# Two-block decoder of 256 tokens on one core: scores of 64-feature heads issued in pairs, filler work spread over the pairs, joined MLP products, gated outputs turned in parts

## The reference, cut to what matters

```python
# first block, layer 0: MoBA (8 heads of 64, ALiBi) beside forgetting attention (8 heads of 64)
s_own = einsum('bhqd,bhld->bhql', qc, ko) * Dh**-0.5 - slopes * rel_o        # causal, one block of 256
s_fox = einsum('bhqd,bhsd->bhqs', qb, k) * scale + cb[..., None] - c         # c = cumsum(log f)
y = concat([ya * silu(ga), yb * silu(gb)]);  x = x + y @ w_out_ab[j]
# first block, layer 1: differential attention (4 heads, two maps of 64, values of 128)
#   beside sliding-window attention with sinks (8 query heads of 64, 2 key heads)
x = x + y @ w_out_cd[j]
# second block, layer i = 0, 1: mixer (0: MLA, 1: stick-breaking), cross attention, MLP
h = h + mem_cross_attn(rmsnorm_2(h, norm_cross[i]), rmsnorm_2(mem, norm_mem[i]), ...)
h = h + square(relu(rmsnorm_2(h, norm_mlp[i]) @ w_in)) @ w_out               # 1024 -> 4096 -> 1024
```

## Time and profile before

| | |
|---|---|
| median of three runs | 1026.99 us (1026.68 to 1027.73) |
| the profiled execution: its time | 1027.6 us |
| the profiled execution: its span in the trace | 1025.8 us, mean granted clock of TensorE 0.985 |
| busy share of the span | PE 96%, PEld 86%, DVE 61%, ACT 53%, POOL 4% |
| DMA | 158.14 MB, mean 154 GB/s |

### The profile page before, as it was taken

How to read it: one execution, slowest core, us unless ns; L and a number is a source line. 1 busy time by engine, 2 the same in 40 slices (tenths; PEclk the granted TensorE clock), 3 DMA queues, 4 the chain that set the end, 5 groups by cost and what they waited for, 6 DMA issues and landing times.

```text
span 1025.8 us, 15748 instructions
## 1 busy us (share of the span) xinstructions
PE 989.2 (96%) x6172; PEld 879.7 (86%) x6172; DVE 627.6 (61%) x1208; ACT 548.2 (53%) x1029; POOL 38.3 (4%) x83
## 2 busy tenths in 40 slices
PE   8899999999999979999999999999999999999997
PEld 7677778787787979887999999899988889999995
DVE  5867545486864476656765555557873658455554
ACT  6575564366684445545744434455673557444352
POOL 4011000001130000000000000000000000000000
PEclk9899989999999989999999999999999999999999
DMA  9776312565332434343556565666435435565551
GB/s 288 218 164 124 124 41 88 163 202 164 123 114 62 122 90 150 124 128 121 182 186 200 173 201 176 235 164 177 152 103 185 146 104 195 176 203 171 198 186 42
DMA packets 114167, 158.14 MB, mean 154 GB/s; under 512 B 13783, under 2 KB 55085, under 8 KB 114093
## 3 DMA queue, kind: packets, MB, share of 16 engines
q1 hardware_dynamic: 113656, 156.56, 49.4%
q10 hardware_dynamic: 436, 0.56, 0.2%
HBM read 156.06 MB, written 1.05 MB: 153 GB/s over the span
## 4 chain that ended last, share of the span: by engine, by line
PE 84%; DVE 6%; ACT 4%; issue 2%; SPq 1%; DMA 1%; DVEq 0%; ACTq 0%
PE bank L475 24%; PE bank L476 24%; PE bank L477 24%; PE bank L613 3%; DVE w_lo L1771 2%; PE bank L638 2%; PE bank L627 2%; PE bank L607 1%; PE bank L529 1%; DMA raw<-in_w_in_ab 1%; ACT xT_hi L1319 1%; SPq L2472 1%; DVE xT_lo L1828 1%; ACT pb L1438 1%; PE bank L592 1%
## 5 line engine op out<-in xcount | busy, mean ns | idle before, releaser
L1771 DVE TENSOR_TENSOR w_lo<-raw,w_hi 128x1024 fp32r<-128x1024 f32 (+2 forms) x292 | 336.2, 1195 | 179.2 <-ACT w_hi L1274 178.9
L1274 ACT CAST w_hi<-raw 128x1024 fp32r<-128x1024 f32 (+2 forms) x292 | 283.4, 1027 | 146.6 <-DMA raw<-in_mlp_w_in 74.2
L475 PE MATMUL bank<-xT_hi,w_hi 128*128 128x256 f32 x784 | 224.5, 286 | 3.0 <-DVE xT_lo L1828 2.0
L476 PE MATMUL bank<-xT_lo,w_hi 128*128 128x256 f32 x784 | 222.5, 284 | 0.0
L477 PE MATMUL bank<-xT_hi,w_lo 128*128 128x256 f32 x784 | 222.5, 284 | 0.0
L475 PE MATMUL bank<-w_hi,xT_hi 128*128 128x512 f32 (+1 forms) x432 | 161.8, 375 | 9.0 <-issue 4.0
L477 PE MATMUL bank<-w_hi,xT_lo 128*128 128x512 f32 (+1 forms) x432 | 157.9, 365 | 0.0
L476 PE MATMUL bank<-w_lo,xT_hi 128*128 128x512 f32 (+1 forms) x432 | 157.8, 365 | 0.0
L475 PEld LDWEIGHTS bank<-xT_hi,w_hi 128*128 128x128 f32 x784 | 151.0, 193 | 4.9 <-issue 3.1
L476 PEld LDWEIGHTS bank<-xT_lo,w_hi 128*128 128x128 f32 x784 | 151.0, 193 | 0.7
L477 PEld LDWEIGHTS bank<-xT_hi,w_lo 128*128 128x128 f32 x784 | 151.1, 193 | 0.0
(11 more groups left out here) (243 smaller groups left out, 1096.8 us busy)
## 6 DMA issues: line engine op xcount, KB each, us to landing
raw<-in_mlp_w_in SPq DMA_DIRECT2D x32, 1024.0 KB, 5.4
raw<-in_mlp_w_out SPq DMA_DIRECT2D x32, 1024.0 KB, 5.1
raw<-in_w_in_ab SPq DMA_DIRECT2D x13, 1024.0 KB, 9.3
raw<-in_w_in_cd SPq DMA_DIRECT2D x13, 1024.0 KB, 5.1
raw<-in_xa_w_kv SPq DMA_DIRECT2D x8, 1024.0 KB, 5.2
raw<-in_sb_w_qkv SPq DMA_DIRECT2D x16, 512.0 KB, 5.1
raw<-in_w_out_ab SPq DMA_DIRECT2D x4, 1024.0 KB, 5.2
raw<-in_w_out_cd SPq DMA_DIRECT2D x4, 1024.0 KB, 5.2
```

Source lines behind the costliest of these rows:

```text
L475: pe.matmul(o, wh, ih, start=start, stop=False, skip_group_check=True)
L476: pe.matmul(o, wh, il, start=False, stop=False, skip_group_check=True)
L1274: nc.scalar.copy(w_hi[:, u % SLOTS, a], raw[:, u % SLOTS, a]).then_inc(hi_ready, 1)
L1771: V.tensor_tensor(w_lo[:, u % SLOTS, a], raw[:, u % SLOTS, a], w_hi[:, u % SLOTS, a].bitcast(F32), ALU.subtract).then_inc(lo_ready, 1)
```

## The change

**Joined MLP products.** `xT_hi` and `xT_lo` become views of one tensor `xT` (chunk, hi/lo, token). In blocks 2 to 7 of both MLPs the new `up` issues two matmuls in place of three: w_hi by both parts at once (512 columns, a whole bank for one feature tile) and w_lo by xT_hi (256 columns, left half). All four banks 4 to 7 serve every such block. ACT copies the right half of a bank (4 x 256 columns), DVE adds the left half (4 adds of 256 columns) and then does relu and square in one operation of 512 columns, twice. Blocks 0 and 1 and all `down` products stay.

**Scores in pairs.** `pipeline` becomes `pairs` on PE, ACT and DVE: the scores of two heads are issued together, for fox heads first both 64-partition parts, then both 2-partition parts. Then come, for each head of the pair before, its transposes, the filler, its values.

**Fillers.** They are spread over the steps anew; the memory's 16 transposes go in two halves to steps 9 and 10, and to banks 2 and 3; output projections are given by token tile.

**Gated outputs in parts.** The second 512 features are turned as 2 chunks, 1 chunk and 1 chunk, the first two during the last heads.

**Early splits.** `part` and `rope_keys` start on the first half of a unit. ACT and DVE split uh0 and uh1 before and between the latent steps.

```diff
-        xT_hi = sb("xT_hi", [P, KC, S], F32R)
-        xT_lo = sb("xT_lo", [P, KC, S], F32R)
+        xT = sb("xT", [P, KC, 2, S], F32R)
+        xT_hi, xT_lo = xT[:, :, 0, :], xT[:, :, 1, :]
...
+        GATE_PARTS = ((0, 2, 4, 3), (2, 1, 5, 5), (3, 1, 6, 7))
...
             def part(key, u, b, first, token_layout, r, only=(0, 1)):
+                take(u, 0 if first else 1)
                 if first:
-                    take(u)
                     begin(key, b)
...
-            def scores(k):
+            def scores(*ks):
+                for k in ks:
+                    begin(("S", k["g"]), 4 + k["g"] % 2)
...
+                if kind == "fox":
+                    for n in range(2):
+                        for k in ks:
+                            o = banks[4 + k["g"] % 2]
+                            for t, (a, z) in enumerate(k["spans"]):
+                                ins = pe.matmul(o[:, a:z], k["parts"][n](t * P, (t + 1) * P), k["keys"][n](0, z - a), ...)
...
+            def pairs(ks, fill):
+                for p in range(len(ks) // 2 + 1):
+                    if 2 * p < len(ks):
+                        scores(*ks[2 * p:2 * p + 2])
+                    for n in range(2):
+                        old = ks[2 * p - 2 + n] if p else None
+                        if p:
+                            turn_probs(old)
+                        for f in fill.get(2 * p + n, []):
+                            f()
+                        if p:
+                            values(old)
...
-                5: [unit("vb", 0), turn("kb", 5, 1)], 6: [unit("vb", 1), fox_rows], 7: [unit("gb", 0)], 9: [unit("gb", 1)],
-                12: [lambda: memory(0)], 13: [lambda: gate("yab0", ...)],
-                14: [mem_part(0)], 15: [mem_part(1)], 17: [half("oab", 0, 0, X, "yab0")], 18: [half("oab", 0, 1, X, "yab0")]})
-            gate("yab1", 7, 4, heads_of("fox")[-1]["output"])
+                5: [unit("vb", 0), turn("kb", 5, 1)], 6: [unit("vb", 1), fox_rows], 7: [unit("gb", 0)], 8: [unit("gb", 1)],
+                9: [lambda: memory(0)], 10: [lambda: memory(1)], 11: [mem_part(0)], 12: [lambda: gate("yab0", ...)],
+                13: [mem_part(1)], 14: [half("oab", 0, 0, X, "yab0", (0,))], 15: [half("oab", 0, 0, X, "yab0", (1,))],
+                16: [half("oab", 0, 1, X, "yab0", (0,)), lambda: gate_part("yab1", 7, 0, heads_of("fox"))],
+                17: [half("oab", 0, 1, X, "yab0", (1,)), lambda: gate_part("yab1", 7, 1, heads_of("fox"))]})
+            gate_part("yab1", 7, 2, heads_of("fox"))
...
-            mem_part(2)()
-            pipeline(heads_of("swa"), {1: [mem_part(3)], 4: gate ycd0, 5, 6, 8, 10: quarters of ocd})
+            pairs(heads_of("swa"), {0: [mem_part(2)], 2: [mem_part(3)], 3: gate ycd0, 4, 5, 6: quarters of ocd,
+                8: [half("ocd", 0, 1, X, "ycd0", (1,)), gate part 0], 9: [gate part 1]})
+            gate_part("ycd1", 6, 2, heads_of("swa"))
...
+                def up(u, blk):
+                    for n in range(2):
+                        take(u + n)
+                        for f in range(4):
+                            b = 4 + f
+                            if n == 0:
+                                pe.wait_ge(relu_ready, relu0 + 4 * (blk - 2) + f + 1)
+                            for c in range(4):
+                                k = 4 * n + c
+                                pe.matmul(banks[b][:, :], wh, xT[:, k].rearrange("p a s -> p (a s)"), start=k == 0, ...)
+                                ins = pe.matmul(banks[b][:, 0:S], wl, xT_hi[:, k, :], stop=k == KC - 1, ...)
...
 ACT and DVE, latents of MLA:
-            x_turned(("x", 0), U["ocd", 1, 1], U["dq", 0], True)
+            x_turned(("x", 0), U["ocd", 1, 1], U["dq", 0])
+            row_copy(("x", 0))
+            used(U["dk", 0])
...
             latent(2)
+            used(U["dp", 0])
             latent(0)
             latent(1)
-            used(U["dk", 0])
-            used(U["dp", 0])
             used(U["dq", 1])
...
 ACT, MLP blocks from 2:
+                    for f in range(4 if blk >= 2 else 0):
+                        nc.scalar.copy(pan(4, f // 2)[:, f % 2 * S:(f % 2 + 1) * S], banks[4 + f][:, S:2 * S]).then_inc(second_ready, 1)
 DVE, MLP blocks from 2:
+                            V.tensor_tensor(o, banks[4 + f][:, 0:S], o, ALU.add).then_inc(relu_ready, 1)
+                        V.scalar_tensor_tensor(out=pan(5, p), in0=pan(4, p), scalar=0.0, in1=pan(4, p), op0=ALU.max, op1=ALU.mult)
```

More of the change, by code:

```diff
@@ L594, in qk_transposes @@
                     end((name, "T", pair), ins, (qkT_ready, state["qkT"]))
-            def scores(k):
[L597 to L602, removed]
-                        pe.wait_ge(fox_ready, 2)
[L604 to L609, removed]
+            def scores(*ks):
+                for k in ks:
+                    begin(("S", k["g"]), 4 + k["g"] % 2)
+                kind = ks[0]["kind"]
+                if kind in qkT_needed:
+                    pe.wait_ge(qkT_ready, qkT_needed[kind])
+                    if kind == "fox":
+                        pe.wait_ge(fox_ready, 2)
+                if kind == "fox":
+                    for n in range(2):
+                        for k in ks:
+                            o = banks[4 + k["g"] % 2]
+                            for t, (a, z) in enumerate(k["spans"]):
+                                ins = pe.matmul(o[:, a:z], k["parts"][n](t * P, (t + 1) * P), k["keys"][n](0, z - a),
+                                                start=n == 0 and t == 0, stop=n == 1, skip_group_check=True)
+                            if n == 1:
+                                end(("S", k["g"]), ins, (logits_ready, k["g"] + 1))
+                    return
+                for k in ks:
+                    o = banks[4 + k["g"] % 2]
@@ L610, in scores @@
                     for t, (a, z) in enumerate(k["spans"]):
-                        keys = z - a
                         for n, (q, kk) in enumerate(zip(k["parts"], k["keys"])):
-                            ins = pe.matmul(banks[b][:, a:z], q(t * P, (t + 1) * P), kk(0, keys),
-                                            start=n == 0, stop=n == len(k["parts"]) - 1)
-                end(("S", g), ins, (logits_ready, g + 1))
+                            ins = pe.matmul(o[:, a:z], q(t * P, (t + 1) * P), kk(0, z - a), start=n == 0, stop=n == len(k["parts"]) - 1)
@@ L822, in gate, with gate_part, gate_chunk, ready @@
                 yr[key] = gated(key, *a)
-            def memory(i):
-                yr["m", i] = turn_mem(i)
+            def gate_part(key, panel, n, ks):
+                first, chunks, b0, last = GATE_PARTS[n]
+                yr[key, n] = gated((key, n), panel, b0, ks[last]["output"], first, chunks)
+            def gate_chunk(key):
+                def ready(k):
+                    n, c = ((0, 0), (0, 1), (1, 0), (2, 0))[k - 4]
+                    return yr[key, n](c)
+                return ready
@@ L830, in _ @@
             half = lambda name, m, n, lhs, key, ts=range(T): lambda: project_half(name, m, n, lhs, yr[key], ts=ts)
[L831 removed]
+            pairs(heads_of("moba") + heads_of("fox"), {
                 0: [unit("qb", 0)], 1: [unit("qb", 1)], 2: [unit("kb", 0)], 3: [unit("kb", 1), turn("qb", 4, 1)], 4: [lambda: row_scales(("n", 0), 1), lambda: fgate(r)],
[L833 to L835 removed]
@@ L2133, in _ @@
             split_to = lambda *key: lambda: used(U[key])
-            pipeline(heads_of("moba") + heads_of("fox"), {
+            pairs(heads_of("moba") + heads_of("fox"), {
                 0: [split_to("qb", 0), lambda: gate_panel("ga")], 1: [split_to("qb", 1), lambda: qk_sums("qb")],
```

175 lines of the change are left out of this document (99 added, 76 removed).

## The result

The changed kernel takes 1015.01 us, the median of four runs (1014.22 to 1018.16), against 1027.36 for the kernel before. The ratio is 0.9886 with a 95% interval of [0.9864, 0.9908]. In a later series it took 1014.96 (ratio 0.9896 [0.9875, 0.9917]). So it is faster, by 12.3 us where 24.3 were forecast, and 1015.0 lies outside the range of 995.5 to 1011.5.

What follows compares the result with a forecast made beforehand. PE was taken to bound nearly everything. Savings of 4.8 (MLP), 13.2 (pairs), 1.4 (tails) and 5.3 (latents), 0 for the slow stretch and 0.4 added for switches gave -24.3 us: 1002.7 for the median, range 995.5 to 1011.5.

Steps and rivals of the forecast that it cites:

- Joined MLP products: Both MLPs: two matmuls replace three, saving 12.5 ns each of 384 times, 4.8 us; bounds 0 and 4.8.
- The cover for ACT and DVE: MLP blocks: banks are free 5 to 6 us after an up, needed after 10.9, so 5 us of cover.
- Scores in pairs: Attention scores: the second head is nearly free; moba and swa pairs save 6.6 us, fox pairs 6.6.
- the choice between the bounds for the 2-partition parts: Fox pairs: the two heads' 2-partition parts overlap, saving 0.85 us a pair; bounds 0 and 0.85.
- Fillers: First attention stage: slow-clock stretch broken up but a new wait made, net 0; bounds 4.8 gained, 3.5 lost.
- The 3.1 + 0.3 us: PE waits 3.1 us before the values of head 8, and 0.3 more at the memory's keys.
- 4.8 back, 4.9 given: Slow stretch: 4.8 us regained from the clock, against new waits of 3.1 and 0.3 and 1.5 of low clock.
- Gated outputs in parts: The two attention tails: PE's waits fall from 4.3 to 2.9 us, saving 1.4; bounds 0 and 3.
- The sliding-window pairs: Sliding-window stage: four pairs of swa scores each save 0.83 us; tail waits of 0.7 at step 7, 0.4 at step 9.
- Early splits: Latents before MLA: the 3.07 us wait and 1.6 of slow clock go, 5.3 us saved in all; bounds 2 and 5.3.
- rival (b): Attention stages: ACT and DVE become the bound, 1.5 us at some five places plus low clock, 1013 us; chance 0.10.
- Rival (e): Score pairs: PE's order keeps the heads apart, all 13.2 us fall away, 1015.9 us; chance 0.04.

Runs made afterwards that it cites:

- join_only: The kernel before with the joined MLP products alone: 1023.46 us against 1025.74, ratio 0.9972.
- fox_by_head: The changed kernel with a fox pair issuing both parts of the first head, then both of the second: 1027.66 us, ratio 1.0022.
- plus_kb: mem_tail_join with ACT's inverse root for kb's norms ahead of head 4's exps and DVE's kb sums ahead of the split: 1004.56 us.
- tail_order: The changed kernel with DVE's split at step 17 dropped from ahead of the last fox head's output and left until later: 1012.61 us.
- mem_tail_join: The changed kernel with the memory's chunks ahead of the gate, join widths grouped, and the tail's split right behind the last fox chunk: 1008.36 us.
- swa_dve: mem_tail_join with DVE's first sliding-window logits ahead of gate gd and the last memory unit's split behind head 0's output: 1001.70 us.
- all_dve: plus_kb with the same DVE order in the sliding-window stage as swa_dve: 1001.39 us, ratio 0.9753.

## Why the prediction was wrong

The sign and the savings on PE's stream were right; what ACT's and DVE's order would do to them was not. By its steps:

- **Joined MLP products: mis-sized.** "I take 4.8" was the upper bound of its own range and the runs show 2.5 alone (join_only) and 2.2 in the changed kernel. The step that failed is that durations measured in blocks of one width hold when the widths alternate: a pair takes 353 ns, not 347, or 6.9 less than three products instead of 12.5 (384 x 6.9 = 2.6 us). Grouping gives back some 0.6 us an MLP. The 1.0 us by the formula of the Trainium skill (TensorE: Matmul & The Clock Gate, Back-to-back issue gap), which the page gives for the isolated gap of a single matmul, is missed on the other side: the traces have 2.2 to 2.5. The cover for ACT and DVE was right: no up waits.
- **Scores in pairs: right**, 0.86 and 1.72 us for pairs where 0.87 and 1.74 were taken. So was the choice between the bounds for the 2-partition parts, and fox_by_head shows what hung on it. One reading beside it is off: the parts of a fox head lie in disjoint partitions for h % 4 = 1 and 2, not for odd heads (the second part starts at 32 * (h % 4)).
- **Fillers: the named wait came, others weren't named.** The 3.1 + 0.3 us came as 2.2 + 0.3 and about 0.6 behind, with the low clock. But the wait at step 5 (2.2) isn't in the prediction: the scaling of kb frees a bank that the unit "vb" needs, and it waits for ACT's inverse root, which stood behind the exps of a head (plus_kb moved it, and 0.9 of the wait went). "4.8 back, 4.9 given" expected one low stretch; there were four between 90 and 182 us, and the clock missing from 1.00 in slices of 2 us from 60 to 232 us adds up to 6.8 us where it was 5.1 before. In the first attention stage the sum leaves PE 1.8 us of waits from before, 3.4 new ones at the memory and 0.7 less in the tail, together 4.5, and it had 8.9; these 4.4 us are over half of the 8.0 missing there, and the rest goes with the clock.
- **Gated outputs in parts: this step failed.** It priced the wait for the last head's output at "0.9 twice (nearest: 0.7 in rows 8)". It was 3.2 in the first tail. A split of 2.35 us stood ahead of that output in DVE's queue, in the code that the prediction had before it, and the sum doesn't price it. The 0.7 of rows 8 doesn't price it either, although a split and a head's logits stand ahead of that output too:

```profile
312.32 2.36 DVE L1771 TENSOR_TENSOR w_lo<-raw,w_hi 128x1024 fp32r<-128x1024 f32 x2 [0.93 <-ACT w_hi L1274]
...
315.80 0.47 DVE L2006 SCALAR_TENSOR_TENSOR arena<-bank,rsum,arena 128x64 f32<-128x64 f32 x2
...
316.33 0.88 PE L638 MATMUL bank<-arena,pt 128*128 128x64 f32 x6 [0.75 <-DVE arena L2006]
```

There DVE began the split 3.3 us before PE ran out of work (316.33 - 0.75 = 315.58); in the tail it began at 175.38, when PE already stood still (178.38 - 3.23 = 175.15). The length of a wait was carried over without what decided it. tail_order and mem_tail_join bring the wait to 1.0.
- **The sliding-window pairs: two waits not named**, 1.6 us for the maxima of the first pair and 1.1 for an output, where the prediction had only 0.7 at step 7 and 0.4 at step 9. The first pair's logits stood behind the gate, the output behind a split (swa_dve).
- **Early splits: right**, 5.4 for 5.3, and the next wait stayed where it was, at 2.7. The 1.6 for the clock in it was luck in part: in join_only the same wait has no low clock behind it.

The range's upper end counts 2 us for the latents where their bounds lie 3.3 apart; with 3.3 it is 1012.9, and 1015.0 lies outside all the same.

So rival (b), with a chance of 0.10 and 1013 us, comes nearest to what happened: DVE and ACT become the bound at some places, and the low clock comes on top, though the waits at step 5, in the tail and for the first sliding-window pair aren't among its five places. Rival (e) has the nearest number, 1015.9, and is excluded: the pairs do what they say. The prediction's case against it, "PE waits little there now", was the weak sentence: that PE waited little while it had 9.9 us more to do says nothing of how far ahead the others were. swa_dve and all_dve, with the order of ACT's and DVE's work as the main edit, come out at 1001.7 and 1001.4 us, where the prediction had 1002.7. That shows that order, and the clock that went with it, could give back as much as was missing; the grouped join holds some 1.2 us of it. It doesn't make the terms right. In all_dve the first attention stage is 12.8 us shorter than before (forecast 10.4, with no low clock left in it, which the sum had not counted on), the second 2.6 (3.8) and the MLPs 3.9 (4.8).

What stays open: why the step from one width to the other costs 6 ns a pair, and why a low clock stretch follows some waits and not others, and once no wait at all. In all_dve waits of 1.4 are still there, and the clock stays at 1.00 up to 334 us.

## What to carry to other kernels

When work is taken off the bounding engine, list for each of its waits to come what stands ahead of the awaited instruction in the other engine's queue, with its length; a 0.48 us output behind a 2.35 us split is priced at 2.8, less what the bounding engine still has to do when the split begins. Put work that is needed only later (splits, casts, a gate) behind what the bounding engine waits for next; in the two runs here that moved fillers on the bounding engine instead, the waits only moved. And a duration measured in a run of equal instructions can be too short where two kinds alternate.

## What the hardware did that was not expected

- The step between a matmul of 512 columns and one of 256 isn't the sum of its parts: 236 + 117 = 353 ns in turn, 227.3 + 119.9 = 347.2 in blocks.
- Parts over 64 and over 2 partitions did not overlap, even in disjoint partitions and different banks: 3.40 us for a fox pair by head, 1.72 with equal parts side by side.
- Taking a wait away gave back more than the wait. Between the changed kernel and mem_tail_join the waits account for 3.4 us of the first stage, and the rest of the 8.0 came with the clock. Where it falls differs from run to run of one kernel: 96, 113, 137 and 178 us in one execution, 134 to 144 and 178 to 185 in another, with the same stage total of 172.6 to 172.7. Behind the same wait of 3.07 us the clock was 0.54 in the kernel before and 1.00 in join_only.
